# Four Strassen pairs in every feed-forward block, with one of each pair's weight sums made by a DMA

## The reference

```python
for l in range(DEPTH):                                   # DEPTH = 2
    h = rmsnorm(x, norm_ffn1[l])
    x = x + 0.5 * (silu(h @ w1) * (h @ w3)) @ w2         # D_FF = 2816
    h = rmsnorm(x, norm_mix[l])
    proj = h @ w_in[l]            # retention q,k,v,gate | window q,k,v | memory q | 3 branch gates
    ret, swa = retention(...), sliding_window_attention(...)
    mkv = rmsnorm(mem, norm_mem[l]) @ w_mem_kv[l]        # 256 memory tokens
    mo = memory_attention(...)
    merged = sum(sigmoid(gate_b) * (branch_b @ w_up_b))  # three branches
    x = x + merged @ w_o[l]
    h = rmsnorm(x, norm_ffn2[l])
    x = x + 0.5 * (silu(h @ w1) * (h @ w3)) @ w2
return rmsnorm(x, norm_final)
```

## Time and profile before

| | before |
|---|---|
| time, median of 3 runs | 1491.39 us (1490.92 to 1491.55) |
| span of the profiled execution | 1489.4 us |
| own time of that execution | not recorded; the median stands 2.0 us above the span |
| PE busy | 1471.5 us, 99% of the span |
| DVE busy | 979.3 us, 66% |
| ACT busy | 829.5 us, 56% |
| POOL busy | 56.8 us, 4% |
| granted TensorE clock | 0.999 |
| bytes moved by DMA | 266.9 MB, 179 GB/s |

### The profile page before, as it was taken

The page is one execution under the profiler, slowest core; times in us unless marked ns, Lnnn a source line. Parts: engine busy times, 40 slices in busy tenths (PEclk is TensorE's granted clock), DMA queues, the critical chain, the costliest instruction groups (busy, mean ns, idle before and its releaser), DMA issues.

```text
span 1489.4 us, 17019 instructions
## 1 busy us (share of the span) xinstructions
PE 1471.5 (99%) x7006; PEld 1221.8 (82%) x7006; DVE 979.3 (66%) x856; ACT 829.5 (56%) x998; POOL 56.8 (4%) x64
## 2 busy tenths in 40 slices
PE   8999999999999999999999999999999999999998
PEld 6888888888888888788788888888888888878886
DVE  6888644564455467888778875546445464688895
ACT  7565555665445437656465654656644554475653
POOL 0000000220000000000000000004000000000000
PEclk9999999999999999999999999999999999999999
DMA  9556345444454465654744445544444544736631
GB/s 370 196 197 249 139 160 187 141 142 141 148 192 142 158 240 195 226 195 167 260 170 151 163 181 198 183 170 141 142 146 166 177 160 144 287 137 226 226 113 43
DMA packets 39293, 266.90 MB, mean 179 GB/s; under 512 B 4433, under 2 KB 5073, under 8 KB 7729
## 3 DMA queue, kind: packets, MB, share of 16 engines
q1 hardware_dynamic: 37392, 259.54, 48.3%
q10 hardware_dynamic: 1552, 5.37, 1.0%
q0 software_dynamic: 272, 0.92, 0.2%
HBM read 264.76 MB, written 1.05 MB: 178 GB/s over the span
## 4 chain that ended last, share of the span: by engine, by line
PE 92%; DVE 3%; ACT 2%; DMA 1%; issue 1%; SPq 0%; POOLq 0%; POOL 0%; ACTq 0%
PE bank L644 28%; PE bank L646 27%; PE bank L645 27%; PE bank L700 4%; DVE w_lo L1343 1%; PE bank L875 1%; PE bank L968 1%; PE bank L951 1%; PE bank L861 1%; ACT w_hi L1028 1%; DMA raw<-in_stream 1%; PE bank L849 1%; DVE raw_more L1341 1%; ACT w_hi_more L1028 1%; ACT prob L1256 0%
## 5 line engine op out<-in xcount | busy, mean ns | idle before, releaser
L1343 DVE TENSOR_TENSOR w_lo<-raw,w_hi 128x2048 fp32r<-128x2048 f32 x165 | 380.2, 2305 | 374.3 <-ACT w_hi L1028 373.7
L1028 ACT ACTIVATE w_hi<-raw 128x2048 fp32r<-128x2048 f32 x165 | 316.0, 1915 | 275.4 <-PE bank L646 267.6
L644 PE MATMUL bank<-w_hi,hT_lo 128*128 128x512 f32 (+1 forms) x984 | 387.4, 394 | 0.8 <-issue 0.3
L646 PE MATMUL bank<-w_lo,hT_hi 128*128 128x512 f32 (+1 forms) x984 | 380.5, 387 | 0.0
L645 PE MATMUL bank<-w_hi,hT_hi 128*128 128x512 f32 (+1 forms) x984 | 379.8, 386 | 0.0
L644 PEld LDWEIGHTS bank<-w_hi,hT_lo 128*128 128x128 f32 x984 | 184.9, 188 | 39.7 <-issue 4.3
L646 PEld LDWEIGHTS bank<-w_lo,hT_hi 128*128 128x128 f32 x984 | 184.8, 188 | 38.3
L645 PEld LDWEIGHTS bank<-w_hi,hT_hi 128*128 128x128 f32 x984 | 185.1, 188 | 35.2
L1343 DVE TENSOR_TENSOR w_lo<-raw_more,w_hi 128x2048 fp32r<-128x2048 f32 x69 | 157.7, 2288 | 27.2 <-ACT w_hi L1028 27.0
L1028 ACT ACTIVATE w_hi<-raw_more 128x2048 fp32r<-128x2048 f32 x69 | 132.2, 1918 | 38.7 <-PE bank L646 28.6
L644 PE MATMUL bank<-w_hi,bT_lo 128*128 128x512 f32 x320 | 126.5, 395 | 0.0
(11 more groups left out here) (188 smaller groups left out, 1973.8 us busy)
## 6 DMA issues: line engine op xcount, KB each, us to landing
raw<-in_stream SPq DMA_DIRECT2D x173, 1024.0 KB, 4.9
raw_more<-in_stream SPq DMA_DIRECT2D x71, 1024.0 KB, 5.1
raw<-in_stream SPq DMA_DIRECT2D x8, 256.0 KB, 7.1
memT<-in_memt ACTq DMA_DIRECT2D x2, 1024.0 KB, 4.9
stB<-in_mem ACTq DMA_DIRECT2D x2, 1024.0 KB, 6.2
x<-in_x SPq DMA_DIRECT2D x2, 256.0 KB, 4.6
x<-in_x SPq DMA_DIRECT2D x1, 512.0 KB, 7.6
decay<-in_decay POOLq DMA_DIRECT2D x1, 512.0 KB, 10.4
```

What stands on the lines that cost most here:

```text
L644: nc.tensor.matmul(dst, xl, wh[:, a:b], start=first, stop=False, skip_group_check=more)
L646: return nc.tensor.matmul(dst, xh, wl[:, a:b], start=False, stop=last, skip_group_check=more)
L1028: nc.scalar.activation(slots(o)[0], raw_slot(s), ACT.Copy).then_inc(hi_split, 1)
L1343: nc.vector.tensor_tensor(lo, raw_slot(s), hi.bitcast(F32), ALU.subtract).then_inc(weights_made, 1)
```

## The change

- Each feed-forward block has four pairs: sixteen in all. The order of each block is written out by hand (`FFN_ORDER`). The products stand in the order 5 1 3 6 2 7 4, but down units, plain units and products of the next pair stand between them.
- The sums of the left operand have other signs, so that a weight sum is an add of one raw slot into another that the sum takes the place of (`raw[to] += raw[plus]`, L1530). Two of the three `half` sums become a scalar_tensor_tensor (L1634).
- The weight sum of product 7 isn't made by DVE: a DMA on POOL's queue adds the other quarter from HBM onto the raw slot (`add_quarters`, L648), 1 MB each, sixteen in all. The high copy of product 7 on ACT waits for it. The sums for 5, 6 and 4 stay with DVE: 48 of them, where there were 40.
- The raw slots: three, and two in the SBUF of `bT_hi` (`raw_b`), and two in that of `rqT`/`rkT` (`raw_q`). `mkT` and `mv` are therefore made elsewhere, stored to HBM and loaded again before they are used: four more DMAs of 1 MB in each layer, on ACT's queue. `S_hi` and `S_lo` have SBUF of their own.
- The mixing part has the same 57 units and steps in another order (`SCHEDULE`).

The core of the diff:

```diff
-SEGMENTS = {1: [(0,),(1,),(2,),(3,4,5),(6,7,8,9),(10,)],
-            2: [(0,),(1,),(2,3,4),(5,6,7),(8,9,10)]}
-PAIRS = {f: [seg for seg in SEGMENTS[f] if len(seg) > 1] for f in (1, 2)}
-WEIGHT = {1: "11", 5: "11", 3: "22", 6: "11", 7: "12", 4: "11", 2: "21"}
-SUMS = {1: ("11", "12", "11"), 2: ("11", "22", "11"), 3: ("12", "22", "12"), 4: ("11", "21", "11")}
-SUM_OF = {5: 1, 6: 2, 7: 3, 4: 4}
+PAIRS = {0: list(dict.fromkeys(s[2] for s in STEPS if s[0] == "prod")),
+         1: [(2, 3), (4, 5), (6, 7), (8, 9)],
+         2: [(2, 3), (5, 6), (7, 8), (9, 10)]}
+FFN_ORDER = {1: """
+u0.0 u0.1 u1.0 g0 u1.1 d0 g1 p0:5 p0:1 p0:3 p0:6 d1 p0:2 p0:7 p1:5 p0:4 g3 p1:3 p1:1 g2 d3 p1:6 p1:2 p1:7 p2:5 d2 p1:4 g5 p2:3 p2:1 g4 p2:6 d5 p2:2 p2:7 p3:5 d4 p2:4 g7 p3:1 p3:3 p3:6 g6 d7 p3:7 p3:2 p3:4 d6 g9 u10.0 g8 u10.1 d9 d8 g10 mix d10
+""".split(), 2: """
...
+WEIGHT = {1: "11", 5: "12", 3: "22", 6: "12", 7: "22", 4: "12", 2: "21"}
+SUMS = {5: "11", 6: "22", 7: "12", 4: "21"}
+SUM_EARLY = {7: 1}
+ADDED = {(1, 0): (7,), (1, 1): (7,), (1, 2): (7,), (1, 3): (7,), (2, 0): (7,), (2, 1): (7,), (2, 2): (7,), (2, 3): (7,)}
...
+            def add_quarters(o):
+
+                for l, pair, m, behind in added_after[o]:
+                    to = raw_of[l, pair, WEIGHT[m]]
+                    pool.wait_ge(raw_loaded[to[0]], 16 * to[1])
+                    if behind:
+                        pool.wait_ge(weights_made, behind)
+                    _, f, k = pair
+                    pool.dma_start(raw_slot(to[0]), stream[l * NU + quarter_unit(f, k, SUMS[m])], accum_op=ALU.add)\
+                        .then_inc(quarter_added[m], 16)
...
-                    to, plus, minus = (raw_of[o // NI, pair, q] for q in SUMS[k])
+                    to, plus = (raw_of[o // NI, pair, q] for q in (WEIGHT[m], SUMS[m]))
+                    dve.wait_ge(raw_loaded[to[0]], 16 * to[1])
                     dve.wait_ge(raw_loaded[plus[0]], 16 * plus[1])
-                    nc.vector.tensor_tensor(raw_slot(to[0]), raw_slot(plus[0]), raw_slot(minus[0]), ALU.subtract)                        .then_inc(weights_made, 1)
+                    nc.vector.tensor_tensor(raw_slot(to[0]), raw_slot(to[0]), raw_slot(plus[0]), ALU.add).then_inc(weights_made, 1)
...
+                    elif s == "mkT_in":
+                        act.wait_ge(*full(l, "mqt_3"))
+                        act.wait_ge(mkT_stored, 16 * (l + 1))
+                        act.dma_start(mkT[:, :, :].rearrange("p k m -> p (k m)"), mkT_kept).then_inc(mkT_back, 16)
```

More of the change, by code:

```diff
@@ new lines @@
+""".split()
+PAIR_OF, STEPS = {}, []
+for _t in SCHEDULE:
+    _head, *_inside = _t.split("+")
+    if ":" in _head:
+        _k, _n = _head.split(":")
+        STEPS.append(("prod", 0, _k, int(_n)))
+        PAIR_OF |= {_c: (_k, _j) for _j, _c in enumerate(MIX_PAIRS[_k])}
+    elif "." in _head:
+        _c, _u = _head.split(".")
+        STEPS.append(("unit", UNIT_AT[_c, int(_u)], _c, int(_u), _c == "skv" or _u == "1", _inside))
+    else:
+        STEPS.append(("step", _head))
+MIX_ITEMS = [s if s[0] == "prod" else ("mix", s[1]) for s in STEPS if s[0] != "step"]
@@ new lines, with added, step @@
+ADDED = {(1, 0): (7,), (1, 1): (7,), (1, 2): (7,), (1, 3): (7,), (2, 0): (7,), (2, 1): (7,), (2, 2): (7,), (2, 3): (7,)}
+def added(pair):
+    return ADDED[pair[1:3]]
+def ffn_steps(f):
+    def step(t):
+        if t == "mix":
+            return "mix", 0
+        kind, rest = t[0], t[1:]
+        if kind == "p":
+            k, n = rest.split(":")
+            return "prod", f, int(k), int(n)
+        if kind == "u":
+            c, h = rest.split(".")
+            return "up", f, int(c), int(h)
+        return {"g": "gt", "d": "down"}[kind], f, int(rest)
+    return [step(t) for t in FFN_ORDER[f]]
@@ L219, in plan_weights @@
         item = ITEMS[o % NI]
-        if item[0] == "prod" and item[3] in SUM_OF:
-            first = ITEMS[(o - 1) % NI] == (*item[:3], 1)
-            sums_first[o - (not first)].append((item[:3], SUM_OF[item[3]]))
+        if item[0] == "prod" and item[3] in SUMS and item[3] not in added(item):
+            sums_first[o - SUM_EARLY.get(item[3], 1)].append((item[:3], item[3]))
     for o in range(EARLY, n):
-        for pair, k in sums_first[o]:
+        for pair, m in sums_first[o]:
             count += 1
-            sum_at[o // NI, pair, k] = count
+            sum_at[o // NI, pair, m] = count
         count += 1
         lo_at[o] = count
-    loads, raw_of, held = [], {}, [(-1, None)] * (RING + RAW_MORE)
+    loads, raw_of, held = [], {}, [(-1, None)] * (RAW_X + 1)
+    added_after, added_at, adds = [[] for _ in range(n)], {}, {m: 0 for m in (5, 6, 7, 4)}
     for o in range(n):
@@ L344, in new @@
             return place(name, shape, dt, at)[0]
-        x = new("x", [P, TT, D])
+        x, x_at = place("x", [P, TT, D])
+        raw_x = new("raw_x", [P, UW], at=x_at)
         hT_hi = new("hT_hi", [P, KT, SEQ], F32R)
@@ L367, in build @@
         act_b = new("act_b", [P, TT, FC], at=b_at + 6144)
-        mkT, m_at = place("mkT", [P, KT, MEM])
-        raw_more = new("raw_more", [P, RAW_MORE, UW], at=m_at)
-        mv = new("mv", [P, TT, D])
         rqT, q_at = place("rqT", [P, RET_H, SEQ])
@@ L550, in _ @@
                     x_part(2)
-            for o, unit, s, (until, owner) in loads[EARLY:]:
+            for o, unit, s, (until, owner), _ in loads[EARLY:]:
                 if until > 0:
@@ L877, in grp_values, with wait_done @@
                     last.then_inc(fullsem(name), 1)
+                def wait_done(*chunks):
+                    for chunk in chunks:
+                        for t in range(TT):
+                            pe.wait_ge(*done_of(l, chunk, t))
                 def step(s):
@@ L889, in step @@
                     elif s == "sqt":
[L890 removed]
+                        wait_done("sq0", "sq1")
                         for j in range(4):
@@ L981, in _ @@
                         continue
+                    if s[0] == "prod":
+                        if not by_h:
+                            by_h.append(s)
+                            pe.wait_ge(x_copied, 4 * sums_no(l, 0) + 2)
+                        product(l, *s[1:])
+                        continue
                     _, i, chunk, half, _, inside = s
                     names = [f"{chunk}t{t}" for t in range(TT)]
+                    hi, lo = (bT_hi, bT_lo) if chunk[0] == "u" or chunk[:2] in ("mk", "mv") else (hT_hi, hT_lo)
+                    if hi is hT_hi and chunk[:2] != "wo":
+                        for h in range(2):
+                            if h not in turned and (chunk == "skv" or half == h):
+                                turned.append(h)
+                                for j in range(2):
+                                    pe.wait_ge(*out_of(l, f"xt{h}_{j}"))
                     if chunk == "skv":
```

552 lines of the change are left out of this document (344 added, 208 removed), and 5 rows, old and new, of the table AFTER.

## The result

The changed kernel takes 1507.47 us in the median of four runs (1506.95 to 1508.07), the kernel before 1491.41 us beside it: a ratio of 1.0108, with a 95% interval from 1.0095 to 1.0121. It is slower by 16 us, 1.1%. The forecast was 1483.7 us with a range up to 1496; sign and range were wrong.

A forecast was written before the change was run, and what follows sets the result against it. PE's matmuls were taken to bound the kernel (PE busy 99%); −16.3 + 4.8 + 4.4 + 3.4 − 4.0 = −7.7 us on the span 1489.4 gave 1483.7 us with 2.0 around it; range 1475 to 1496.

The forecast's parts named there:

- PE's gain, −16.3 us: Feed-forward blocks: six more pairs, each with 12 matmuls fewer at 0.2267 us, −16.3 us on PE.
- The pairs, +4.8 us: Runs of pairs: DVE needs 31.0 us a pair to PE's 30.6; 0.4 charged on twelve pairs, +4.8 us.
- The start, +4.4 us: Start of layer 0: one weight sum ahead of `gT_lo` delays d0 2.2 us, the next delays `S_lo`; +4.4 us, once.
- `mg0`, +3.4 us: Mixing part: `mg0` now follows um0.1 at once, so PE waits 1.7 us for `merged` in each layer, +3.4 us.
- The waits that went, −4.0 us: Feed-forward blocks: two PE waits on `gT_lo` and one on `act_a` vanish with the new order, −4.0 us.
- The clock: PE: clock stays at the 2.4 GHz level since PE stays as busy as before, so no term.
- The add, 9.8 us, hidden: POOL's queue: a 1 MB add takes 9.8 us, twice a plain load, hidden in 10.6 us of room.
- The second, DVE as the bound with hand-offs: Runs of pairs: DVE becomes the bound, 0.6 us more for each of twelve pairs, +7.2, 1490.9 us; chance 0.12.
- The third, late adds: Pairs: late POOL adds hold ACT's copies, then DVE and PE; slower from an add of 11.1 us; chance 0.21.
- The signs: Wrong if adds exceed 11 us, DMA idles ACT before product 7's copy, `w_lo` waits exceed 12, or `mkT` reloads late.

The follow-up runs named there:

- the four kernels of the table: The change with 64, 48 (unaltered), 32 (second DMA add a pair) or 32 (product 4's sum left out) weight sums on DVE: 1525.26, 1507.47, 1490.95, 1488.18 us.
- order_a: The changed kernel with feed-forward items reordered to put more PE work between two products of a pair that write bank 7: 1535.27 us.
- reads_first: The changed kernel with DVE's read of bank 7 put ahead of the previous item's splits at four places of each first feed-forward block: 1511.52 us.
- plain_dma: The changed kernel with a plain load in place of the accumulating DMA on POOL's queue, product 7's sum left out: 1505.98 us.

## Why the prediction was wrong, point by point

- **PE's gain, −16.3 us**: as stated; 72 matmuls fewer.
- **The pairs, +4.8 us** is the step that failed: "How much of the 0.4 gets through ... 12 x 0.4". It measured +25.0 us. The balance of DVE's work to PE's was right (88.2 to 86.6 us in the run of the first block), but a sum over a pair isn't what PE waits for. Two things were left out. The balance was drawn for a pair with two down units, while the order puts stretches of products with none between (p1:5 p0:4 g3 p1:3 p1:1), where each 2.7 us of PE asks for a split of 2.2 and every few products for a sum, a half and gated halves besides; what DVE falls behind there it hasn't done ahead, and the 4.95 us that it idles later (before 149.7) don't give it back. (This reading of the order is argued from the timeline; no run tries it apart.) And I looked only for weights and `gT_lo` as what PE would wait for, not for PSUM banks: bank 7, which four products of a pair share (17.6 us of the waits), and bank 4, where a product follows an up unit (4.2 us). That DVE's load decides is shown by the four kernels of the table, with 16 sums more or fewer. The two kernels with another order (order_a, reads_first) didn't gain, but both also made the adds late, so they don't rule out that another order would. How the two parts of the cause, the load and the short distance, share the 25 us is only bounded: some 6 us of waits at short distances stay when a third of the sums is gone.
- **The start, +4.4 us**: the first half of it, d0 later by a weight sum, measured 2.4 as a wait, and as much again since 12 matmuls of d0 then ran at half clock. The second, for `S_lo`, shows as no wait in the changed kernel, where d0 ran at half clock in part (from 36.5 to 41.7 us) and PE came late itself; in the kernel with two adds a pair alone, where it didn't, PE waited 1.9 us for `S_lo`. So the two together cost about what the term says.
- **`mg0`, +3.4 us**: right as a wait, 1.6 us in each layer, 3.5 with the restarts; undoing it brought 3.8 us in one kernel, and 1.6 in another, within the intervals.
- **The waits that went, −4.0 us**: right, −4.5.
- **The clock** was said not to enter. It did, with 5.2 us: 14 matmuls at half clock behind two waits of the pairs (2.8 us), and 12 behind the wait at the start (2.4).
- **The add, 9.8 us, hidden**: 8.4 to 8.9 measured. It wasn't hidden everywhere: ACT waited for it seven times, 9.6 us in sum, of which little reached PE (plain_dma). In the second pair the chain of DVE's work does lead through it: the sum for product 6 ends at 76.1, and the chain of waits goes on

```profile
76.61 9.03 DMA raw_q<-in_stream
85.64 0.02 issue
85.67 1.93 ACT w_hi_more L1145
```

  ACT had waited 2.7 us, and DVE 1.2. I had given this pair 11.5 us from PE's side; on DVE's side only three splits, a sum and small work follow, 10.4 us, which less ACT's copy leave the add 8.4.
- **The rivals.** The second, DVE as the bound with hand-offs, at a chance of 0.12, was the mechanism, and its price of 7.2 us was too small by a factor of nearly three: the pairs cost 20.2 us more than the forecast's 4.8. The third, late adds, at 0.21, has the right side for the wrong reason in this kernel, and came true where the order was changed (order_a). The prediction took the Trainium skill ("SBUF — State Buffer", section "Who interferes with whom") to speak for late adds, since a GpSimd DMA can be held up by VectorE. The same section says that a probe saw `tensor_copy` stall the DMA and `tensor_tensor` not, and the splits and sums here are `tensor_tensor`. The trace agrees: beside a DVE that was busy 98.7% of 89 us, the plain loads from POOL's queue took 5.2 us, as SP's did (4.9 to 5.3), and the adds 7.7 to 9.4.
- **The signs.** Of the four that were to show the prediction wrong, one came: ACT's idle time ahead of product 7's copy was put down to a DMA. No add took over 11 us (the slowest 9.4), PE had no wait for `w_lo`, and the reload of `mkT` took 5.4 and 5.9 us, with no wait for it.

## What to carry to other kernels

An average balance between two engines says whether a stretch can be hidden, not whether it will be. Lay the second engine's work against the first over each stretch as short as the lookahead (here four items), and count the banks that several steps share among what can be waited for. When an engine becomes full, the places where others wait for it move about; taking work away helped (35 us of DVE gave 17 to 19 us here), while the two new orders for the reads didn't, and made a third engine's waits longer besides. A unit of independent work between a producer and the transposes that need its result is worth its place in the order (`mg0`). Moving one instruction has to be followed on every engine that waits for it, not only on its own.

## What the runs showed of the hardware

An accumulating DMA of 1 MB from HBM onto SBUF took 8.4 to 8.9 us in the medians by slot, where a plain one on the same queue took 5.2; with twice as many adds 9.3 to 11.2, and up to 14.1 for a single one. After some waits of PE the granted clock fell to the lower of its two levels, 1.2 GHz, for 3 us. Behind the wait of 2.12 us at 627.78, PE's timeline and then two windows (in the windows the column after POOL's busy time is the clock):

```profile
629.02 0.53 PE L743 MATMUL bank<-w_lo,hT_hi 128*128 128x512 f32 x1
629.35 0.63 PE L741 MATMUL bank<-w_hi,hT_lo 128*128 128x512 f32 x1
629.77 0.63 PE L742 MATMUL bank<-w_hi,hT_hi 128*128 128x512 f32 x1
...
632.66 0.39 PE L743 MATMUL bank<-w_lo,S_hi 128*128 128x512 f32 x1
```

```profile
628.00:632.00 4.00, 4.00 (x13) 3.10 (x13) 4.00 (x3) 0.00 (x0) 0.00 (x0) 0.64 0.83 328
...
636.00:640.00 4.00, 4.00 (x19) 3.30 (x19) 4.00 (x5) 1.61 (x2) 0.00 (x0) 1.00 0.13 53
```

Matmuls start every 0.43 us there in place of 0.23, and the wait of 2.1 us costs some 1.5 us more. A wait of the same length in layer 1, at 1370 us, had no such sequel. So a wait can cost more than its bracket. The kernels with many waits also scatter more from run to run (9 us in order_a, under 1 in the kernel before), which fits that.
